# Decay differences of an SSD scan on the vector engine, with two exponentials of 2048 elements in place of 32 of 128

## The reference, cut to what matters

```python
acum = jnp.cumsum(a_, axis=1)
seg = acum[:, :, None] - acum[:, None, :]
decay = jnp.exp(jnp.where(lower, seg, -jnp.inf))
cb = jnp.einsum('bign,bjgn->bijg', c_, b_)
y_intra = jnp.einsum('bijg,bijgr,bjgr,bjgrp->bigrp', cb, decay, dt_, x_)
```

## Time and profile before

| | us |
|---|---|
| median of 3 runs | 2269.93 |
| lowest and highest | 2265.98, 2270.43 |
| profiled execution, its own time | 2270.54 |
| its span, first to last instruction | 2268.7 |
| PE busy | 2133.5 (94%) |
| DVE busy | 1458.6 (64%) |
| ACT busy | 1231.6 (54%) |
| POOL busy | 47.8 (2%) |

### The profile page before, as it was taken

How to read it: one execution, slowest core, us unless ns; L and a number is a source line. 1 busy time by engine, 2 the same in 40 slices (tenths; PEclk the granted TensorE clock), 3 DMA queues, 4 the chain that set the end, 5 groups by cost and what they waited for, 6 DMA issues and landing times.

```text
span 2268.7 us, 27496 instructions
## 1 busy us (share of the span) xinstructions
PE 2133.5 (94%) x11320; PEld 1720.4 (76%) x11320; DVE 1458.6 (64%) x1392; ACT 1231.6 (54%) x1373; POOL 47.8 (2%) x20
## 2 busy tenths in 40 slices
PE   6889999979899999999878999999999999999997
PEld 4677878767677777878567887888878787888875
DVE  3567777753333323225646888878878887888884
ACT  4567666652322222224645767666767676675763
POOL 0011111100000000000000000000000000000000
PEclk9999999979899999999988999999999999999998
DMA  8233445432245444332315999999999999999990
GB/s 305 95 117 145 140 155 181 175 112 75 84 157 174 161 170 160 109 110 96 131 54 213 361 341 339 346 352 331 358 338 345 333 342 345 341 359 335 345 338 21
DMA packets 137732, 509.61 MB, mean 225 GB/s; under 512 B 15296, under 2 KB 15680, under 8 KB 135296
## 3 DMA queue, kind: packets, MB, share of 16 engines
q1 hardware_dynamic: 137520, 507.65, 62.7%
q10 hardware_dynamic: 80, 0.13, 0.0%
HBM read 504.45 MB, written 3.28 MB: 224 GB/s over the span
## 4 chain that ended last, share of the span: by engine, by line
PE 81%; DVE 8%; ACT 4%; issue 1%; DVEq 0%; ACTq 0%
PE ps L1076 14%; PE ps L1074 14%; PE ps L1075 14%; PE ps L654 10%; PE ps L656 10%; PE ps L655 10%; DVE area L1783 3%; DVE d_lo L1654 2%; PE ps L1060 1%; PE ps L1133 1%; ACT area L1315 1%; PE ps L1103 1%; PE ps L666 1%; PE ps L751 1%; ACT d_hi L1247 1%
## 5 line engine op out<-in xcount | busy, mean ns | idle before, releaser
L2102 DVE TENSOR_TENSOR w_lo<-w_raw,w_hi 128x2048 fp32r<-128x2048 f32 x336 | 749.3, 2285 | 51.7 <-ACT w_hi L1537 50.8
L1537 ACT ACTIVATE w_hi<-w_raw 128x2048 fp32r<-128x2048 f32 x336 | 625.8, 1918 | 79.0 <-PE ps L1076 78.2
L1654 DVE TENSOR_TENSOR d_lo<-d_raw,d_hi 128x2048 fp32r<-128x2048 f32 (+1 forms) x76 | 171.9, 2262 | 333.8 <-ACT d_hi L1247 333.8
L1074 PE MATMUL ps<-w_hi,x_hi 128*128 128x512 f32 x896 | 357.1, 399 | 2.0 <-DVE x_lo L2158 2.0
L654 PE MATMUL ps<-h_top,d_hi 128*128 128x512 f32 (+1 forms) x816 | 331.5, 406 | 25.5 <-DVE h_low L1646 9.8
L1076 PE MATMUL ps<-w_hi,x_lo 128*128 128x512 f32 x896 | 355.0, 396 | 0.0
L1247 ACT ACTIVATE d_hi<-d_raw 128x2048 fp32r<-128x2048 f32 (+1 forms) x76 | 143.7, 1890 | 381.8 <-DMA d_raw<-in_dense 244.3
L1075 PE MATMUL ps<-w_lo,x_hi 128*128 128x512 f32 x896 | 350.7, 391 | 0.0
L656 PE MATMUL ps<-h_top,d_lo 128*128 128x512 f32 (+1 forms) x816 | 322.9, 396 | 0.0
L655 PE MATMUL ps<-h_low,d_hi 128*128 128x512 f32 (+1 forms) x816 | 319.3, 391 | 0.0
L654 PEld LDWEIGHTS ps<-h_top,d_hi 128*128 128x128 f32 x816 | 158.3, 194 | 69.9 <-issue 26.2
(11 more groups left out here) (275 smaller groups left out, 2493.2 us busy)
## 6 DMA issues: line engine op xcount, KB each, us to landing
w_raw<-in_experts SPq DMA_DIRECT2D x672, 512.0 KB, 5.6
d_raw<-in_dense SPq DMA_DIRECT2D x240, 512.0 KB, 5.2
area<-acum_rows SPq DMA_DIRECT2D x16, 1024.0 KB, 8.4
d_raw<-in_dense SPq DMA_DIRECT2D x8, 384.0 KB, 4.0
xT<-in_xt SPq DMA_DIRECT2D x4, 512.0 KB, 6.7
gate_rows<-area SPq DMA_DIRECT2D x4, 512.0 KB, 6.8
hT<-gate_rows SPq DMA_DIRECT2D x2, 1024.0 KB, 5.9
cst<-in_consts SPq DMA_DIRECT2D x2, 512.0 KB, 10.9
```

Source lines behind the costliest of these rows:

```text
L1074: mm(o, hi, w_hi[u % HIGH][:, a:a + 512], start=first, stop=False)
L1537: A(w_hi[n % HIGH][:], w_raw[n % RAW][:], ACT.Copy).then_inc(S["whi_done"], 1)
L1654: TT(d_lo[u][:, 0:w], d_raw[u][:, 0:w], d_hi[si % D_HIGH][:, 0:w].bitcast(F32), ALU.subtract)\
L2102: TT(w_lo[n % RAW][:], w_raw[n % RAW][:], w_hi[n % HIGH][:].bitcast(F32), ALU.subtract)\
```

## The change

The addition of `nb` moves from the bias of the exponentials to the vector engine. For each group DVE forms rowb + nb in eight additions over 4 heads x 128 tokens (one per direction and chunk, with `nb` broadcast along the tokens) into `seg`; POOL then selects in place; ACT takes one exponential of 2048 elements per direction. A new semaphore, `seg_op`, counts the directions, and the waits for `rowb_in` and `y_ready` move from POOL to DVE.

```diff
         def _(pl):
             for g in range(GROUPS):
-                pl.wait_ge(S["rowb_in"], 32 * g + 32)
-                if g:
-                    pl.wait_ge(S["y_ready"], 2 * g)
                 for d in range(2):
-                    pl.affine_select(out=seg[d].rearrange("p h (c i) -> p (h c) i", c=NCH),
-                                     in_=rowb[d].rearrange("p h (c i) -> p (h c) i", c=NCH),
-                                     compare_op=ALU.is_ge, fill=-1e30, base=0,
+                    pl.wait_ge(S["seg_op"], 2 * g + d + 1)
+                    v = seg[d].rearrange("p h (c i) -> p (h c) i", c=NCH)
+                    pl.affine_select(out=v, in_=v, compare_op=ALU.is_ge, fill=-1e30, base=0,
...
             def segments(g):
-                if not g:
-                    act.wait_ge(S["nb_op"], 2)
                 for d in range(2):
                     act.wait_ge(S["seg_mask"], 2 * g + d + 1)
-                    for h in range(HPG):
-                        for ch in range(NCH):
-                            v = seg[d][:, h, ch * P:ch * P + P]
-                            j = 32 * d + 4 * g + h
-                            last = A(v, v, ACT.Exp, bias=nb[:, ch, j:j + 1])
-                    last.then_inc(S["e_done"], 1)
+                    A(seg[d], seg[d], ACT.Exp).then_inc(S["e_done"], 1)
...
+            def segments(g):
+                dv.wait_ge(S["rowb_in"], 32 * g + 32)
+                if g:
+                    dv.wait_ge(S["y_ready"], 2 * g)
+                for d in range(2):
+                    o = seg[d].rearrange("p h (c i) -> p h c i", c=NCH)
+                    i0 = rowb[d].rearrange("p h (c i) -> p h c i", c=NCH)
+                    for ch in range(NCH):
+                        a = per_token(nb, d, g)[:, ch, :].unsqueeze(2).to_broadcast([P, HPG, P])
+                        last = TT(o[:, :, ch, :], i0[:, :, ch, :], a, ALU.add)
+                    last.then_inc(S["seg_op"], 1)
...
                     group_inverse(g - 1)
+                if not g:
+                    dv.wait_ge(S["nb_op"], 2)
+                segments(g)
                 dense_low(3 * g + 4)
...
             gate_low(0)
             finish(6)
+            segments(7)
             token_scales(7)
```

More of the change, by code:

```diff
@@ L485, in backbone @@
             dt_ps dt_v dt_act dt_dve dt_tr dt_tok ac_ps ac_sb ac_exp ac_tail ac_rows ac_rows_sb scr_out
-            gemm_evac tap_done conv_step cx_ready tr_ready tok_evac xs_ready st_ready st_op seg_mask
+            gemm_evac tap_done conv_step cx_ready tr_ready tok_evac xs_ready st_ready st_op seg_op seg_mask
             er_done m_add gspread nb_op nb_ln e_done m_done ce_done y_ready sk_done ys_done yg_done ysq_done gsum_done grs_done grinv_done gT_done
```

## The result

The changed kernel takes 2275.72 us, the median of 7 runs (2275.11 to 2277.09); the kernel before took 2268.43 us beside it (7 runs, 2264.78 to 2270.43). The ratio is 1.0033, with a 95% interval of 1.0022 to 1.0045: 7.3 us slower. The profiled execution of the changed kernel spans 2273.3 us, that of before 2268.7. These two differ by 4.6 us only, since the rows of group 0 land 2.3 us earlier in the changed kernel's trace (102.33 for 104.64), behind code that is the same in both. That part varies from one execution to the next: over the 14 traces of this study the DMA that sends these rows is issued between 92.58 and 96.00 us.

A forecast was written before the change was run, and what follows sets the result against it. Matrix work was 81% of the chain; late selects would delay the evacuation TensorE waits for. 2.5 (g = 1, 4) + 2.4 (g = 2, 3, 5, 6) + 0.0 + 3.9 + 1.5 = 10.3 us on 2269.9: 2280.2, range 2267 to 2288.

The forecast's parts named there:

- undisturbed behind the additions: Rival: GpSimd gets in after the additions, selects end at T+10.05 and T+12.0; +0.4 us, 2270.3 us; chance 0.18.
- The rival without holding-off: Additions never hold GpSimd off; selects end at T+7.8 and T+10.2; -3.3 us, 2266.6 us; chance 0.10.
- The rival of the clock: Each group exposes a 1.2 GHz stretch on TensorE: six at 1.55 us instead of one, 2288 us; chance 0.14.
- 1.9 taken: Scalar engine: each exponential of 2048 elements was assumed to take 1.9 us, from a copy of that size.
- 4.9 taken: Vector engine: eight additions of 512 elements were put at 4.9 us a group.
- The table load: Scalar engine: assumed ahead of the wait for the select; behind it, +1.3 us a group, a sign against the forecast.
- the main line: GpSimd is held off until the weights' split ends at T+10.4; selects finish at T+12.25 and T+14.2; chance 0.58.
- the variant of one instruction only: First select enters between additions at T+6.35; additions and split end two us later, second select T+14.3; same sum.
- g = 0: First group: evacuation to 118.5, TensorE now starts at 118.49 and will again: 0.0 us.
- g = 7: Last group: no product hides the chain, token scaling at 478.35 instead of 474.49: +3.9 us.
- g = 1 to 6: Evacuation at T+17.15 sets a period of 51.2 us: +1.25 each for g = 1 and 4, +0.6 each for the others.
- Clock: TensorE's gap in g = 1 and 4 grows to about 1.9 us; one exposed 1.2 GHz stretch taken: +1.5 us.

The follow-up runs named there:

- e2: The changed kernel with both directions signalled to GpSimd only after all eight additions: 2275.86 us, ratio 1.0028 to the kernel before.
- e1: The changed kernel with selects first, from the landed rows, and additions in place on their output: 2263.28 us, ratio 0.9973 to the kernel before.
- e9: The select-first kernel, with group 7's additions moved forward: direction 0 ahead of its reciprocal, direction 1 behind it: 2259.64 us, ratio 0.9954 to the kernel before.
- e7: The changed kernel with one addition of 2048 elements per direction instead of four of 512: 2272.24 us (one run).
- e5: The changed kernel with each addition written as scalar_tensor_tensor, rows x 1.0 + nb: 2278.41 us (one run).
- e6: The changed kernel with each addition waiting by semaphore for the one before last: 2274.84 us (one run).
- e8: The changed kernel with the additions of groups 0 to 6 behind the split and finish, as in group 7: 2309.57 us (one run).
- e11: As e9, with one addition of 2048 elements per direction instead of four of 512: 2257.97 us, ratio 0.9952 to the kernel before.
- e10: As e9, with direction 0's additions ahead of the reciprocal in groups 1 to 6 too: 2262.82 us, ratio 0.9969 to the kernel before.

## Why the prediction was right, point by point

**Sign, place and size.** Forecast 2280.2 in a range of 2267 to 2288, measured 2275.72. By the mechanism of the forecast: the selects are late because they wait for vector work, and the evacuation, which TensorE waits for, is late with them. The trace carries this through the groups: TensorE starts the bc product at T+16.92 to T+16.94 in groups 1 to 6, just behind the evacuation's end at T+16.88, where before it started at T+15.95 or T+16.5 to 16.6.

No rival came whole. GpSimd didn't run undisturbed behind the additions. The rival without holding-off has the first select's end at T+7.8, and in groups 1 to 6 it nearly is there (T+8.1); but the second, on which the time depends, was held and ends at T+13.95 instead of T+10.2. The rival of the clock has a stretch in every group: there is one, but none of it shows in the period.

**Durations.** Two exponentials of 1.92 us each (1.9 taken); additions 4.90 us in group 7 and 4.83 in e2 (4.9 taken). The table load stands ahead of the wait, as taken: between the select's end and the exponential there are 0.04 us.

**GpSimd held off.** In group 7 as forecast. In groups 0 to 6 the main line was wrong on the first select, which wasn't held until the split's end. What came was the variant of one instruction only, which the prediction took from the Trainium skill (SBUF — State Buffer, "Who interferes with whom"): first select in between two additions (forecast to start at T+6.35; it started about 1.86 us before 160.91, that is T+6.3), additions and split later by its hold, second select T+14.3 (measured T+13.95). That the sum is the same by both was said beforehand and was right, so the wrong step cost nothing; e2 shows it as an experiment.

**Group by group.** g = 0: 0.0 forecast, 0.1 less measured. g = 7: +3.9 forecast, +3.86 measured. g = 1 to 6: 4.9 forecast, 3.4 measured. The term that was mis-sized is the evacuation's end: T+16.88 instead of T+17.15. Six times 0.27 is 1.6. About half of it is the order: e2, where the first select does wait for the split as in the main line, has periods of 51.09 us, where the forecast has 51.2 and the change 50.94 (the hold is 1.8 us and not the two of the variant). The rest is overlap: consecutive rows overlap by 0.07 to 0.08 us (the additions' row ends at 162.67, the split starts at 162.59), which the sum counted twice. One reading was wrong without harm: the period from T of group 6 to T of group 7 is 48.4 us before, not 50.6; what the change adds there, 0.36 us, is as in groups 2, 3 and 5 (0.33, 0.34, 0.42).

**Clock.** +1.5 forecast, 0 measured: the step that failed. I had TensorE's gap ahead of bc grow to 1.9 us in two groups and be followed by the lower level, on the loop. It is 0.25 us in group 1, where the earlier trace rows has 0.67. What I missed is that the same groups could fall into the other pattern: in all six groups now the gap of 1.47 us (at 152.99 in group 1) is followed by matmuls at the 1.2 GHz level (0.80 us for the first at 154.01, where the earlier trace rows has 0.50 at 155.90). Why all six fell into it, no run shows. So TensorE finishes x late and hardly waits for the evacuation. The stretch lies where there was slack, and costs nothing; the windows show it, 0.98 where the earlier trace rows has 1.00. So the two kinds of period became one, set by the evacuation.

**The level.** The forecast was counted from 2269.9 us, the runs beside the change put before at 2268.43. Of the 4.5 us between forecast and measurement 1.5 are this, 1.5 the clock and 1.5 groups 1 to 6.

**What I left unasked.** The prediction priced the change as written and never asked which half of it costs. The selects stood beside the convolutions, for nothing; the change gave that up for an order that the arithmetic doesn't need. e1 keeps the additions and exponentials of the change and is 6.5 us faster than before.

## What to carry to other kernels

When work moves from one engine to another, count the hand-overs on the waiting chain, not the busy time: here 45 us less on the scalar engine and 50 more on the vector engine bought 7 us of loss in one order and 6.5 us of gain in the other (e1), 10 with the last group's additions moved forward too (e9). Leave the step with the longest private wait (here GpSimd's select) where its input first exists, and put the new step behind it. Before filling an engine's idle time, look at what the other engine does in it: a gap on the vector engine during a GpSimd instruction is no gap for work that reads two SBUF tensors.

## What was not expected of the hardware

- GpSimd and the vector engine alternate by single instructions in some places (e7: addition, select, split, select, each held 1.8 to 2.1 us by the one before) and not in others (group 7: three boundaries between additions pass while the select waits, and it ends 1.84 us after the last). Neither the kind of instruction (e5) nor waits between them (e6) decide, nor does the moment of the request, as far as the trace tells (0.22, 0.23 and 0.31 us into an addition); with small additions, a finish directly ahead goes with the second behaviour (e8). The rule stays open.
- The hold works both ways and costs 1.8 us for a select of 2.0: the split on 128x2048 took 4.09 us instead of 2.28, four additions 4.27 instead of 2.43.
- One vector instruction of 2048 elements with a broadcast operand takes 2.22 us (e11, 454.16) where four of 512 need 2.43 (e9 and e10).
- 128x2048 exponentials take 1.92 us; the 16 small ones for the same elements took 4.7.
